# Attention scores of a 128-token tile in four visits of the tensor engine (6, 6, 4 and 4 PSUM banks) instead of five of 4

## The chip, the cores and the metric

The kernel runs on all 8 NeuronCores of one Trainium2 chip. The batch of 16 samples is split two to a core, and the cores do not talk to each other. The time is the device time in microseconds of the slowest core. The kernel before takes 2286.27 us (median of 3 runs, 2286.07 to 2286.58).

## The reference, cut to what matters

One layer: a modulated RMSNorm, one wide input projection, a pooling branch A, an attention branch B over a window of 128 tokens to either side plus 256 context keys, gates, output projection, RMSNorm and residual. The change touches the scores of branch B alone:

```python
Q_BLOCK = 128; WINDOW = 128; N_HEADS = 16; N_KV_HEADS = 4; HEAD_DIM = 64
def block(i):
    qb = q[block i]                     # (B, 128, KV, G, D)
    kb = k[blocks i-1, i, i+1]          # 384 latent keys
    s_lat = einsum('bqhgd,bkhd->bhgqk', qb, kb) * scale       # masked to |q - k| <= 128
    s_ctx = einsum('bqhgd,bkhd->bhgqk', qb, k_ctx) * scale    # 256 context keys
    p = softmax(concatenate([s_lat, s_ctx, sink_col]))
    return p_lat @ vb + p_ctx @ v_ctx
# in bf16 matmuls here; x (16, 4096, 1024), ctx (16, 256, 1024)
```

So a tile of 128 queries meets three latent blocks of 128 keys (left, own, right) and two context blocks: five key blocks. The first and the last tile of a sample have one latent block less, and so four. The left and the right block need a mask, the own block and the context blocks need none.

## The kernel before, in words

Each core works through 64 tiles (32 to a sample, two samples) in `period(p)`. All engines run programs whose order is that in which the Python code records the operations; `Tracker.emit` works out the semaphore waits. An instruction of PE (the tensor engine) never waits for another one of PE, since `_need` skips that pair. There is no scheduler: what stands first in `period` runs first on its engine. There are 8 PSUM banks of 128 x 512 f32; `next_bank` gives the one whose last use in program order is oldest.

A score visit (`visit`, matmuls at L740) treats one key block. The contraction is over 32 rows, twice (x = 0, 1, the two halves of a rotated head), so four key-value heads g = 0..3 sit in four row groups of 32 rows of the PE array and their matmuls run side by side. A visit is 8 matmuls, 512 query columns each (4 query heads x 128 queries), into 4 banks, one per g. ScalarE (ACT) then takes the exponential of each bank into the tile PT (L743), and VectorE (DVE) masks it where needed (L753), one visit later in the program (`pend`). All other matmuls use all 128 rows.

A period on PE, for tile p, in order: visit 1 (left block); K and V projection of tile p+1 (`P_kv`: 16 matmuls of 128 columns at L580, then 8 of 256 at L573); a gate block (`gm`, 8 of 512, L573); visit 2 (own block); `A_mm` (4, L804); two output blocks of tile p-2 (`out_mm`, 16, L870); visit 3 (right block); `P_xa` (32 of 128 columns, L580); a gate block; visit 4 (context 0); `P_q` (64 of 128 columns, L580); visit 5 (context 1); `B_mm` (8, L812), gate, `A_mm`; probabilities times values (`pv`, L766) with a gate block between; `B_mm`, the silu gate blocks. The right block's keys kT are made in the same period: P_kv on PE, two multiplications on DVE (L607, L609), two additions on GpSimd (POOL, L612). P_kv reads eight slices of hT that DVE writes late in the period before (`norm_mod`, L532).

Of the kernel before, what the change touches and what calls it, by code (L numbers as in the profile page):

```python
# [10 lines left out]
AF = mybir.ActivationFunctionType  # L11
# [5 lines left out]
CTX = 256  # L17
# [16 lines left out]
class Tracker:  # L34
# [27 lines left out]
                    if kn.get(k2, 0) < v2:  # L62
                        kn[k2] = v2

    def emit(self, eng, fn, reads=(), writes=(), inc=True, dma_sem=None):
        waits = {}
        self.opn += 1
        for b in reads:
            b.touch = self.opn
        for b in writes:  # L70
            b.touch = self.opn
        for b in reads:
            self._need(eng, b.last_w, waits)
            if b.excl:
                for r in b.readers:
                    if r[0] != eng:
                        self._need(eng, r, waits)
        for b in writes:
            self._need(eng, b.last_w, waits)
            for r in b.readers:  # L80
                self._need(eng, r, waits)
        self._apply_waits(eng, waits)
        if dma_sem is not None:
            self.count[dma_sem] = self.count.get(dma_sem, 0) + 16
            ev = (dma_sem, self.count[dma_sem])
            incspec = (dma_sem, 16)
        elif inc:
            self.count[eng] = self.count.get(eng, 0) + 1
            ev = (eng, self.count[eng])
            incspec = (eng, 1)  # L90
        else:
            ev = (eng, self.count.get(eng, 0) + 1)
            incspec = None
        self.snap[ev] = dict(self.known[eng])
        for b in reads:
            b.readers.append(ev)
        for b in writes:
            b.last_w = ev
            b.readers = []
        self.ops[eng].append((sorted(waits.items()), fn, incspec))  # L100
        return ev
# [61 lines left out]
def build_program(L, STOP=0):  # L163
    NT = L // 128
# [28 lines left out]
    E = tr.emit  # L193
# [6 lines left out]
    def view(t, off, dims):  # L200
        a = t[:]
        return AP(a.tensor, a.offset + off, [[a.ap[0][0], 128]] + [list(d) for d in dims])

    def pview(t, p0, pn, off, dims):
        a = t[p0:p0 + pn]
        return AP(a.tensor, a.offset + off, [[a.ap[0][0], pn]] + [list(d) for d in dims])

    with es:
# [4 lines left out]
        def sb(name, shape, dt, stack=es):  # L213
            return stack.enter_context(nc.sbuf_tensor("s_" + name, list(shape), dt))
# [17 lines left out]
        kTc = [sb(f"kTc{i}", [128, 2, CTX], BF16) for i in range(2)]  # L232
# [6 lines left out]
        qT = [sb(f"qT{i}", [128, 2, 4, 128], BF16) for i in range(2)]  # L239
        scr = [sb(f"scr{i}", [128, 512], F32) for i in range(NS)]  # L240
        ub = sb("ub", [128, 512], F32)
        kT = [sb(f"kT{i}", [128, 2, 128], BF16) for i in range(NR)]
# [9 lines left out]
        PT = sb("PT", [128, 5, 4, 512], BF16)  # L252
# [12 lines left out]
        def _lru(bufs):  # L265
            i = min(range(len(bufs)), key=lambda j: bufs[j].touch)
            tr.opn += 1
            bufs[i].touch = tr.opn
            return i

        def next_bank():
            i = _lru(pbuf)
            return pbank[i], pbuf[i]
# [3 lines left out]
        def bf(name):  # L277
            if name not in B:
                B[name] = Buf(name)
            return B[name]  # L280
# [94 lines left out]
        def gate_block(h):  # L375
# [15 lines left out]
          reads=[bf("sc"), bf("cT")], writes=[bf("sc")])  # L391
# [325 lines left out]
        def blocks_of(t):  # L717
            i = t % NT
            out = []
            if i > 0:  # L720
                out.append(("lat", (t - 1) % NR, 0))
            out.append(("lat", t % NR, None))
            if i < NT - 1:
                out.append(("lat", (t + 1) % NR, 1))
            out += [("ctx", 0, None), ("ctx", 1, None)]
            return out

        def visit(t, jb):
            kind, idx, mk = blocks_of(t)[jb]
            b = (t // NT) % 2  # L730
            q = qT[t % 2]
            banks = [next_bank() for g in range(4)]
            for x in range(2):
                for g in range(4):
                    if kind == "lat":
                        lk, kb = pview(kT[idx], 32 * g, 32, x * 128, [[1, 128]]), bf(f"kT{idx}")
                    else:
                        lk, kb = pview(kTc[b], 32 * g, 32, x * CTX + idx * 128, [[1, 128]]), bf(f"kTc{b}_{idx}")
                    rq = pview(q, 32 * g, 32, x * 512, [[1, 512]])
                    E("pe", lambda e, lk=lk, rq=rq, g=g, x=x: e.matmul(out=banks[g][0][:, :], lhsT=lk, rhs=rq, start=(x == 0), stop=(x == 1)),  # L740
                      reads=[kb, bf(f"qT{t % 2}_{x}")], writes=[banks[g][1]], inc=(x == 1))
            for g in range(4):
                E("act", lambda e, g=g: e.activation(out=PT[:, jb, g, :], in_=banks[g][0][:, :], func=AF.Exp, scale=0.125),  # L743
                  reads=[banks[g][1]], writes=[bf(f"PT{jb}_{g}")] + ([bf(f"st{jb - 2}")] if t == 0 and jb in (2, 3) else []))

        def mask(t, jb):
            mk = blocks_of(t)[jb][2]
            if mk is None:
                return
            for hh in range(2):  # L750
                v = view(PT, (jb * 4 + 2 * hh) * 512, [[128, 8], [1, 128]])
                bs = [bf(f"PT{jb}_{2 * hh}"), bf(f"PT{jb}_{2 * hh + 1}")]
                E("dve", lambda e, v=v: e.tensor_tensor(out=v, in0=v, in1=view(maskb, mk * 128, [[0, 8], [1, 128]]), op=ALU.min),  # L753
                  reads=bs + [bf("maskb")], writes=bs)
# [152 lines left out]
        def period(p):  # L907
            hasA, hasG, hasP, hasO = 0 <= p < TT, 0 <= p - 1 < TT, 0 <= p + 1 < TT, 0 <= p - 2 < TT
            nxt = p >= 0 and p + 2 < TT
            nb = len(blocks_of(p)) if hasA else 0  # L910
            visits = iter(range(nb))
            pend = []

            def vis():
                for m in pend:
                    mask(p, m)
                pend.clear()
                jb = next(visits, None)
                if jb is not None:
                    visit(p, jb)  # L920
                    pend.append(jb)

            if p == 1:
                load_gg(0)
            if hasO:
                load_res(p - 2)
            vis()
            if hasP:
                P_kv(p + 1)
            if hasG:  # L930
                tm = gm(p - 1, 7)
            vis()
            if hasG:
                u = A_mm(tm, 0)
            if hasO:
                so = [out_mm(p - 2, nb_) for nb_ in range(2)]
                out_stat(p - 2)
                if (p - 1) % NT == 0 and p - 1 < TT:
                    load_gg((p - 1) // NT)
            vis()  # L940
            if hasP:
                P_xa(p + 1)
            if hasG:
                tm = gm(p - 1, 8)
            vis()
            if hasO:
                out_evac(p - 2, so)
            if nxt:
                norm_sq()
            q = P_q(p + 1) if hasP else iter(())  # L950
            next(q, None)
            if nxt:
                norm_rs()
            next(q, None)
            if p + 2 < TT:
                load_rope(p + 2)
            vis()
# [24 lines left out]
            if hasA:  # L982
                ga(p)
                do_ybT(p)
            if hasP:
                gb(p + 1, 0)
            if nxt:
                mod_lat(p + 2, range(4, 8))
            if hasG:
                do_mgT(p - 1)  # L990
            if hasP:
                gb(p + 1, 1)
            if hasA:
                pool2(p, res)
# [54 lines left out]
        q = P_q(0)  # L1049
# [127 lines left out]
```

How the kernel before makes its waits and increments, by code:

```python
    def replay_engine(self, eng, eobj, sems):  # L121
        for waits, fn, incspec in self.ops[eng]:
            for key, val in waits:
                eobj.wait_ge(sems[key], val)
            if fn is None:
                continue
            ins = fn(eobj)
            if incspec is not None:
                ins.then_inc(sems[incspec[0]], incspec[1])
```

## Time and profile before

| | |
|---|---|
| median of 3 runs | 2286.27 us |
| profiled execution: its time | 2285.58 us |
| profiled execution: span of the slowest core | 2282.4 us |
| spans of the eight cores | 2279.7 to 2282.5 us |
| PE busy | 2229.5 us, 98% |
| DVE / ACT / POOL busy | 1446.9 / 1198.0 / 733.7 us |
| mean granted clock of PE | 0.993 to 0.994 on every core |

The execution's own time is 3.2 us above its span: what lies around the first and the last instruction. A steady period takes 33.68 us. PE's busy time counts each matmul from its start to a modelled end, so it overlaps with the next one's; the distance from one start to the next start is what a matmul really costs the stream.

### The profile page before, as it was taken

How to read it: one execution, taken by the hardware profiler on the slowest of the kernel's cores; microseconds unless marked ns; L12 is line 12 of the kernel's file. 1: busy time of each engine (PE TensorE's matmuls, PEld its weight loads, DVE VectorE, ACT ScalarE, POOL GpSimd, SP SyncE). 2: the span in 40 equal slices, each digit the busy share in tenths (PEclk: the TensorE clock that was granted, in tenths of full speed). 3: DMA queues.
4: the chain of work that ended last, by engine and by line, in shares of the span. 5: the costliest groups of instructions: out<-in, count | busy, mean ns of one | idle time of the engine just before them, and what ended most of it. 6: DMA issues, size and time to landing. Idle time of an engine off the chain costs nothing.

```text
span 2282.4 us, 64875 instructions; the slowest of 8 cores (2279.7 to 2282.5 us)
## 1 busy us (share of the span) xinstructions
PE 2229.5 (98%) x23312; PEld 1320.8 (58%) x23312; DVE 1446.9 (63%) x3896; ACT 1198.0 (52%) x2325; POOL 733.7 (32%) x852
## 2 busy tenths in 40 slices
PE   6789999999999999999999999999999999999998
PEld 1465565565565556556556556555655655655654
DVE  0456666666666666666666666666666666666664
ACT  1256556555555555555644655555555564565553
POOL 0232333333233233233333323323323323333332
PEclk9899999999999999999999999999999999999999
DMA  9991332332333343333333233334333323323312
GB/s 245 227 178 45 80 77 69 78 81 70 73 89 71 73 80 71 73 80 76 71 78 90 66 77 89 71 70 83 71 73 80 75 71 78 80 68 76 80 45 66
DMA packets 234303, 193.64 MB, mean 85 GB/s; under 512 B 197492, under 2 KB 205812, under 8 KB 231432
## 3 DMA queue, kind: packets, MB, share of 16 engines
q1 hardware_dynamic: 231544, 168.45, 31.3%
q0 software_dynamic: 2448, 21.04, 5.0%
q8 instruction: 195, 3.19, 0.6%
q14 instruction: 116, 0.95, 0.1%
HBM read 125.02 MB, written 33.56 MB: 69 GB/s over the span
## 4 chain that ended last, share of the span: by engine, by line
PE 94%; DMA 2%; DVE 1%; ACT 1%; issue 1%; POOL 0%; SPq 0%; another core or an unknown queue 0%; DVEq 0%; POOLq 0%; ACTq 0%
PE pb L573 31%; PE pb L580 23%; PE pb L812 10%; PE pb L870 10%; PE pb L740 7%; PE pb L766 6%; PE pb L804 5%; DMA s_PT<-x 2%; PE pb L354 1%; DVE s_yb L775 0%; ACT s_PT L743 0%; PE pb L526 0%; POOL s_kT L612 0%; DVE s_hT L532 0%
## 5 line engine op out<-in xcount | busy, mean ns | idle before, releaser
L573 PE MATMUL pb<-s_W,s_hT 128*128 128x512 bf16 (+1 forms) x3584 | 771.5, 364 | 0.0
L743 ACT ACTIVATE s_PT<-pb 128x512 bf16<-128x512 f32 x1264 | 652.5, 605 | 74.4 <-PE pb L740 73.6
L580 PEld LDWEIGHTS pb<-s_hT,s_W 128*128 128x128 bf16 x9216 | 525.2, 98 | 105.3 <-issue 82.7
L580 PE MATMUL pb<-s_hT,s_W 128*128 128x128 bf16 x9216 | 571.8, 220 | 1.4 <-DVE s_hT L532 0.5
L573 PEld LDWEIGHTS pb<-s_W,s_hT 128*128 128x128 bf16 x3584 | 337.9, 98 | 309.6 <-issue 1.7
L793 ACT ACTIVATE s_Tm<-pb 128x512 bf16<-128x512 f32 x256 | 153.1, 598 | 389.4 <-PE pb L573 308.3
L645 DVE TENSOR_TENSOR s_scr<-pb,s_ropet 128x512 f32<-128x512 f32 x256 | 165.0, 686 | 143.4 <-PE pb L580 142.9
L612 POOL TENSOR_TENSOR s_kT<-s_scr 128x128 bf16<-128x128 f32 x128 | 93.6, 731 | 474.7 <-DVE s_scr L609 449.8
L816 POOL TENSOR_TENSOR s_mg<-s_ub,s_scr 128x512 bf16<-128x512 f32 x128 | 161.9, 1265 | 255.3 <-DVE s_scr L797 255.3
L812 PE MATMUL pb<-s_wmf,s_ybT 128*128 128x512 bf16 x1024 | 242.5, 380 | 0.0
L775 DVE SCALAR_TENSOR_TENSOR s_yb<-pb,s_small,s_Gb 128x64 bf16<-128x64 f32 x1024 | 220.1, 277 | 28.3 <-DVE s_small L772 1.3
L870 PE MATMUL pb<-s_wmf,s_mgT 128*128 128x512 bf16 x1008 | 227.8, 379 | 0.0
L876 DVE TENSOR_TENSOR s_scr<-pb,s_gg 128x512 f32<-128x512 f32 x128 | 88.6, 692 | 182.2 <-ACT s_ttmp L873 179.4
L753 DVE TENSOR_TENSOR s_PT<-s_PT,s_maskb 128x1024 bf16<-128x1024 bf16 x248 | 181.5, 753 | 30.4 <-ACT s_PT L743 21.9
L532 DVE TENSOR_SCALAR s_hT<-s_hT,s_gs,s_sh 128x128 bf16<-128x128 bf16 x496 | 183.8, 434 | 0.0
L766 PEld LDWEIGHTS pb<-s_Vr,s_PT 128*128 128x128 bf16 x3008 | 161.9, 98 | 29.7
L797 DVE SCALAR_TENSOR_TENSOR s_ub<-s_Tm,pb 128x512 f32<-128x512 bf16 x128 | 88.0, 688 | 143.7 <-PE pb L804 135.0
L673 ACT ACTIVATE s_ttmp<-pb 128x512 bf16<-128x512 f32 x64 | 38.3, 598 | 262.4 <-PE pb L580 262.4
L650 POOL TENSOR_TENSOR s_qT<-s_scr 128x512 bf16<-128x512 f32 x128 | 160.0, 1271 | 44.3 <-DVE s_scr L645 44.3
L883 POOL TENSOR_TENSOR s_small<-s_small,s_mh 128x1 f32<-128x1 f32 x64 | 65.4, 1021 | 333.5 <-DVE s_small L881 333.5
L870 PEld LDWEIGHTS pb<-s_wmf,s_mgT 128*128 128x128 bf16 x1008 | 98.7, 98 | 118.9
L766 PE MATMUL pb<-s_Vr,s_PT 128*128 128x65 bf16 x3008 | 165.6, 193 | 0.0
(115 smaller groups left out, 2183.1 us busy)
## 6 DMA issues: line engine op xcount, KB each, us to landing
s_xr<-x SPq DMA_DIRECT2D x63, 512.0 KB, 4.9
y<-s_xr SPq DMA_DIRECT2D x63, 512.0 KB, 2.7
s_xt<-x SPq DMA_DIRECT2D x62, 512.0 KB, 4.6
s_W<-w_in POOLq DMA_DIRECT2D x10, 1024.0 KB, 32.0
s_ropet<-rope SPq DMA_DIRECT2D x64, 128.0 KB, 2.0
s_wmf<-w_mod SPq DMA_DIRECT2D x2, 2048.0 KB, 13.5
s_W<-w_mod SPq DMA_DIRECT2D x2, 2048.0 KB, 27.6
s_wmf<-w_mod POOLq DMA_DIRECT2D x2, 2048.0 KB, 17.9
```

The costliest lines, as they stand in the source:

```text
L532: E("dve", lambda e, k=k: e.tensor_scalar(out=dst[:, k, :], in0=(dst[:, k, :] if src is None else src[:, k * 128:(k + 1) * 128]), scalar1= ...
L573: E("pe", lambda e, k=k: e.matmul(out=pb[:, c0:c0 + n], lhsT=h[:, k, :], rhs=W[:, wblk, k, c0:c0 + n], start=(k == 0), stop=(k == 7)), rea ...
L580: E("pe", lambda e, c=c, k=k: e.matmul(out=pb[:, c * 128:(c + 1) * 128], lhsT=W[:, wblk, k, c * 128:(c + 1) * 128], rhs=h[:, k, :], start= ...
L645: E("dve", lambda e: e.tensor_tensor(out=view(s, 0, [[128, 4], [1, 128]]), in0=view(pbx, 0, [[128, 4], [1, 128]]), in1=view(rp, cs * 128, ...
L650: E("pool", lambda e: e.tensor_tensor(out=view(q, x * 512, [[1, 512]]), in0=a[0][:], in1=b_[0][:], op=op), reads=[a[1], b_[1]], writes=[bf ...
L743: E("act", lambda e, g=g: e.activation(out=PT[:, jb, g, :], in_=banks[g][0][:, :], func=AF.Exp, scale=0.125), reads=[banks[g][1]], writes= ...
L753: E("dve", lambda e, v=v: e.tensor_tensor(out=v, in0=v, in1=view(maskb, mk * 128, [[0, 8], [1, 128]]), op=ALU.min), reads=bs + [bf("maskb" ...
L766: E("pe", lambda e, r=r, jb=jb, rv=rv: e.matmul(out=ob[:, r * 128:r * 128 + 65], lhsT=PT[:, jb, g, r * 128:(r + 1) * 128], rhs=rv, start=( ...
L775: E("dve", lambda e, r=r, co=co: e.scalar_tensor_tensor(out=yb[:, co:co + 64], in0=ob[:, r * 128:r * 128 + 64], scalar=small[:, rc + r:rc ...
L812: E("pe", lambda e, k=k: e.matmul(out=pbk[:, :], lhsT=ybT[:, k, :], rhs=Wb[:, k, rd * 512:(rd + 1) * 512], start=(k == 0), stop=(k == 7)), ...
L816: E("pool", lambda e: e.tensor_tensor(out=mg[:, rd * 512:(rd + 1) * 512], in0=u[0][:], in1=v[0][:], op=ALU.add), reads=[u[1], v[1]], write ...
L870: E("pe", lambda e, k=k: e.matmul(out=pb[:, :], lhsT=src[:, k, :], rhs=Wo[:, k, nb * 512:(nb + 1) * 512], start=(k == 0), stop=(k == 7)), ...
```

## The change

A tile with five key blocks now has four visits. The own block has no visit any more: its query columns 0..255 of each head go along with the left block, and columns 256..511 with context block 0. Such a visit has 8 matmuls of 512 columns (`F`) and 8 of 256 (`H`) and fills 6 banks: four for F, and two in which the halves of g = 0, 1 and of g = 2, 3 lie side by side. Two row groups must not write one bank at once, so H of g = 1 and 3 runs early, and the first H of g = 0 and of g = 2 waits on PE's own semaphore until the H matmul of its partner has ended (`after`). The visits are at the places 1, 3, 4 and 5 of the period: left + half, context 0 + half, right, context 1. Nothing is left at place 2. The masks still go with the next place. ACT takes the exponentials of the halves as two instructions of 512 elements, so it has 20 to a tile as before. In the first tile of a sample place 2 is empty too, and the right block moves behind context 0. The last tile of a sample keeps its order.

```diff
-    def emit(self, eng, fn, reads=(), writes=(), inc=True, dma_sem=None):
+    def emit(self, eng, fn, reads=(), writes=(), inc=True, dma_sem=None, after=None):
         waits = {}
+        if after is not None:
+            waits[after[0]] = after[1]
...
-        def visit(t, jb):
+        def visit(t, jb, half=None):
...
+            hbanks = [next_bank() for i in range(2)] if half else []
...
+                if hb is None:
+                    bk, rq, dst = banks[g], pview(q, 32 * g, 32, x * 512, [[1, 512]]), banks[g][0][:, :]
+                    inc = x == 1
+                else:
+                    bk, rq = hbanks[g // 2], pview(q, 32 * g, 32, x * 512 + hb * 256, [[1, 256]])
+                    dst = bk[0][:, (g % 2) * 256:(g % 2) * 256 + 256]
+                    inc = x == 1
+                ev = E("pe", lambda e: e.matmul(out=dst, lhsT=lk, rhs=rq, start=(x == 0), stop=(x == 1)),
+                  reads=[kb, bf(f"qT{t % 2}_{x}")], writes=[bk[1]], inc=inc,
+                       after=done.get(g + 1) if hb is not None and g % 2 == 0 and x == 0 else None)
+                if hb is not None and g % 2 == 1 and x == 1:
+                    done[g] = ev
...
+                seq_ = [F(0, 0), H(1, 0), F(2, 0), H(3, 0), H(1, 1), H(3, 1), F(0, 1), F(1, 0), F(2, 1), F(3, 0),
+                        H(0, 0), F(1, 1), H(2, 0), F(3, 1), H(0, 1), H(2, 1)]
...
+            for g in ((0, 2, 1, 3) if half else range(4)):
...
+            if half:
+                for i in range(2):
+                    o = view(PT, (hj * 4 + 2 * i) * 512 + hb * 256, [[512, 2], [1, 256]])
+                    E("act", lambda e, i=i, o=o: e.activation(out=o, in_=view(hbanks[i][0], 0, [[256, 2], [1, 256]]), func=AF.Exp, scale=0.125),
...
-            visits = iter(range(nb))
+            if nb == 5:
+                plan = [(0, (1, 0)), None, (3, (1, 1)), (2, None), (4, None)]
+            elif p % NT == 0:
+                plan = [(0, None), None, (2, None), (1, None), (3, None)]
+            else:
+                plan = [(0, None), (1, None), (2, None), (3, None)]
```

What stands on PE at the first visit of a tile before the change; `s_kT` and `s_qT` are keys and queries, `s_hT` is the normalised input of the next tile, and the names behind "waits" are the engines waited for:

```order
L740 MATMUL pb<-s_qT,s_kT 128x512 [waits dve]
L740 MATMUL pb<-s_qT,s_kT 128x512 [waits act]
L740 MATMUL pb<-s_qT,s_kT 128x512 [waits dve] x2
L740 MATMUL pb<-s_qT,s_kT 128x512 x4
L580 MATMUL pb<-s_hT,s_W 128x128 [waits dve] x8
L580 MATMUL pb<-s_hT,s_W 128x128 x8
```

The same place with the change, to the last matmul of the visit:

```order
L753 MATMUL pb<-s_qT,s_kT 128x512 [waits dve]
L753 MATMUL pb<-s_qT,s_kT 128x256 [waits dve]
L753 MATMUL pb<-s_qT,s_kT 128x512
L753 MATMUL pb<-s_qT,s_kT 128x256 [waits act,dve]
L753 MATMUL pb<-s_qT,s_kT 128x256 x2
L753 MATMUL pb<-s_qT,s_kT 128x512 x4
L753 MATMUL pb<-s_qT,s_kT 128x256 [waits pe]
L753 MATMUL pb<-s_qT,s_kT 128x512
L753 MATMUL pb<-s_qT,s_kT 128x256 [waits pe]
L753 MATMUL pb<-s_qT,s_kT 128x512
L753 MATMUL pb<-s_qT,s_kT 128x256 x2
```

Two matmuls of 256 columns now wait for PE itself. Behind the visit stands P_kv, whose first four matmuls have lost their waits but for the first, while the next four keep one each:

```order
L582 MATMUL pb<-s_hT,s_W 128x128 [waits act,dve]
L582 MATMUL pb<-s_hT,s_W 128x128 x3
L582 MATMUL pb<-s_hT,s_W 128x128 [waits dve] x4
L582 MATMUL pb<-s_hT,s_W 128x128 x8
L575 MATMUL pb<-s_W,s_hT 128x256 x8
```

For comparison, the third visit of the core's second tile as it stands before the change, where the second matmul has no wait and the third and the fourth have one each:

```order
L740 MATMUL pb<-s_qT,s_kT 128x512 [waits act,pool]
L740 MATMUL pb<-s_qT,s_kT 128x512
L740 MATMUL pb<-s_qT,s_kT 128x512 [waits act] x2
L740 MATMUL pb<-s_qT,s_kT 128x512 x4
```

With the change this place has a context visit with half of the own block, and the right block's visit comes one place later.

The first tile of a sample on PE with the change, from its first visit on; before, the second visit stood with `s_kT` directly behind the eight matmuls of 256 columns (`s_kTc` are the context keys):

```order
L753 MATMUL pb<-s_qT,s_kT 128x512 x8
L582 MATMUL pb<-s_hT,s_W 128x128 x16
L575 MATMUL pb<-s_W,s_hT 128x256 x8
L753 MATMUL pb<-s_qT,s_kTc 128x512 x8
L582 MATMUL pb<-s_hT,s_W 128x128 x32
L753 MATMUL pb<-s_qT,s_kT 128x512 x8
L582 MATMUL pb<-s_hT,s_W 128x128 x64
L753 MATMUL pb<-s_qT,s_kTc 128x512 x8
```

The visit that needs the freshly made keys has moved behind one context visit and the 32 matmuls of P_xa.

## Rows read from the trace of the kernel before

**Rows 1.** The page, parts 1 and 4: busy time by engine, and the chain.

```profile
PE 2229.5 (98%) x23312; PEld 1320.8 (58%) x23312; DVE 1446.9 (63%) x3896; ACT 1198.0 (52%) x2325; POOL 733.7 (32%) x852
PE 94%; DMA 2%; DVE 1%; ACT 1%; issue 1%; POOL 0%; SPq 0%; another core or an unknown queue 0%; DVEq 0%; POOLq 0%; ACTq 0%
```

**Rows 2.** Timeline of PE, one period: start, length to modelled end, line, operands, count.

```profile
985.36 0.61 PE L740 MATMUL pb<-s_qT,s_kT 32*128 32x512 bf16 x8
985.90 1.19 PE L580 MATMUL pb<-s_hT,s_W 128*128 128x128 bf16 x16
...
991.03 3.62 PE L870 MATMUL pb<-s_wmf,s_mgT 128*128 128x512 bf16 x16
...
995.13 1.96 PE L580 MATMUL pb<-s_hT,s_W 128*128 128x128 bf16 x32
...
998.75 0.61 PE L740 MATMUL pb<-s_qT,s_kTc 32*128 32x512 bf16 x8
999.29 3.75 PE L580 MATMUL pb<-s_hT,s_W 128*128 128x128 bf16 x64
1002.97 0.61 PE L740 MATMUL pb<-s_qT,s_kTc 32*128 32x512 bf16 x8
...
1019.04 0.61 PE L740 MATMUL pb<-s_qT,s_kT 32*128 32x512 bf16 x8
```

**Rows 3.** Groups by form: busy us, mean ns of one.

```profile
L740 PE MATMUL pb<-s_qT,s_kTc 32*128 32x512 bf16 x1024 | 78.2, 379 | 0.0
L573 PE MATMUL pb<-s_W,s_hT 128*128 128x256 bf16 x512 | 66.4, 273 | 0.0
```

**Rows 4.** The chain of waits, 1190 to 1195 us, as start, length, what.

```profile
1192.47 0.46 POOL s_kT L612
1192.94 0.14 issue
1193.07 0.61 PE pb L740 x8
```

**Rows 5.** Timeline of PE at the third visit of the second tile.

```profile
148.75 0.84 PE L740 MATMUL pb<-s_qT,s_kT 32*128 32x512 bf16 x8 [0.35 <-POOL s_kT L612]
149.53 0.34 PE L580 MATMUL pb<-s_hT,s_W 128*128 128x128 bf16 x3
```

**Rows 6.** Timeline of PE, P_kv in three of 63 tiles, the first and last among them.

```profile
116.88 1.07 PE L580 MATMUL pb<-s_hT,s_W 128*128 128x128 bf16 x16
...
681.92 1.54 PE L580 MATMUL pb<-s_hT,s_W 128*128 128x128 bf16 x16
...
2199.64 1.22 PE L580 MATMUL pb<-s_hT,s_W 128*128 128x128 bf16 x16
```

**Rows 7.** Timeline of DVE around P_kv of rows 2.

```profile
985.30 0.98 DVE L532 TENSOR_SCALAR s_hT<-s_hT,s_gs,s_sh 128x128 bf16<-128x128 bf16 x4
```

**Rows 8.** Timeline, first tile of the core: PE, with what ended its idle time.

```profile
121.91 0.61 PE L740 MATMUL pb<-s_qT,s_kT 32*128 32x512 bf16 x8 [3.09 <-POOL s_kT L612]
...
123.33 3.46 PE L580 MATMUL pb<-s_hT,s_W 128*128 128x128 bf16 x32 [0.38 <-ACT s_PT L743]
126.72 0.68 PE L740 MATMUL pb<-s_qT,s_kTc 32*128 32x512 bf16 x8
```

**Rows 9.** Windows: busy of each engine, granted clock, DMA.

```profile
123.30:126.90 3.60, 3.57 (x36) 3.36 (x40) 1.39 (x2) 3.16 (x7) 0.00 (x0) 0.53 0.97 162
```

**Rows 10.** Timeline of ACT and PE late in the first tile.

```profile
130.48 1.05 ACT L482 ACTIVATE s_xsb<-s_xt 128x1024 bf16<-128x1024 f32 x1
...
133.97 0.61 PE L526 MATMUL pb<-s_ident,s_xsb 128*128 128x128 bf16 x8 [0.96 <-ACT s_xsb L494]
```

**Rows 11.** Timeline of PE, second visit of the second sample's first tile.

```profile
1193.07 0.61 PE L740 MATMUL pb<-s_qT,s_kT 32*128 32x512 bf16 x8 [1.29 <-POOL s_kT L612]
```

**Rows 12.** Timeline of ACT in the period of rows 2.

```profile
994.75 0.60 ACT L873 ACTIVATE s_ttmp<-pb 128x512 bf16<-128x512 f32 x1 [1.04 <-PE pb L870]
...
995.33 2.05 ACT L743 ACTIVATE s_PT<-pb 128x512 bf16<-128x512 f32 x4
```

More of the change, by code:

```diff
@@ L726, in blocks_of @@
             return out
-        def visit(t, jb):
-            kind, idx, mk = blocks_of(t)[jb]
+        def visit(t, jb, half=None):
             b = (t // NT) % 2
             q = qT[t % 2]
+            bl = blocks_of(t)
             banks = [next_bank() for g in range(4)]
[L733 to L742, printed above, removed]
-                E("act", lambda e, g=g: e.activation(out=PT[:, jb, g, :], in_=banks[g][0][:, :], func=AF.Exp, scale=0.125),
-                  reads=[banks[g][1]], writes=[bf(f"PT{jb}_{g}")] + ([bf(f"st{jb - 2}")] if t == 0 and jb in (2, 3) else []))
@@ new lines, in visit, with st, mm @@
+            hbanks = [next_bank() for i in range(2)] if half else []
+            def st(j):
+                return [bf(f"st{j - 2}")] if t == 0 and j in (2, 3) else []
+            def mm(g, x, j, hb):
+                kind, idx, mk = bl[j]
+                if kind == "lat":
+                    lk, kb = pview(kT[idx], 32 * g, 32, x * 128, [[1, 128]]), bf(f"kT{idx}")
+                else:
+                    lk, kb = pview(kTc[b], 32 * g, 32, x * CTX + idx * 128, [[1, 128]]), bf(f"kTc{b}_{idx}")
+                if hb is None:
[10 more added lines that the diff above has]
+                    done[g] = ev
@@ new lines, in visit @@
+            done = {}
+            if half is None:
+                seq_ = [(g, x, jb, None) for x in range(2) for g in range(4)]
+            else:
+                hj, hb = half
+                F = lambda g, x: (g, x, jb, None)
+                H = lambda g, x: (g, x, hj, hb)
+                seq_ = [F(0, 0), H(1, 0), F(2, 0), H(3, 0), H(1, 1), H(3, 1), F(0, 1), F(1, 0), F(2, 1), F(3, 0),
+                        H(0, 0), F(1, 1), H(2, 0), F(3, 1), H(0, 1), H(2, 1)]
+            for a in seq_:
+                mm(*a)
@@ new lines, in visit @@
+            for g in ((0, 2, 1, 3) if half else range(4)):
+                E("act", lambda e, g=g: e.activation(out=PT[:, jb, g, :], in_=banks[g][0][:, :], func=AF.Exp, scale=0.125),
+                  reads=[banks[g][1]], writes=[bf(f"PT{jb}_{g}")] + st(jb))
+            if half:
+                for i in range(2):
+                    o = view(PT, (hj * 4 + 2 * i) * 512 + hb * 256, [[512, 2], [1, 256]])
+                    E("act", lambda e, i=i, o=o: e.activation(out=o, in_=view(hbanks[i][0], 0, [[256, 2], [1, 256]]), func=AF.Exp, scale=0.125),
+                      reads=[hbanks[i][1]], writes=[bf(f"PT{hj}_{2 * i}"), bf(f"PT{hj}_{2 * i + 1}")] + st(hj))
@@ L910, in period @@
             nb = len(blocks_of(p)) if hasA else 0
-            visits = iter(range(nb))
+            if nb == 5:
+                plan = [(0, (1, 0)), None, (3, (1, 1)), (2, None), (4, None)]
+            elif p % NT == 0:
+                plan = [(0, None), None, (2, None), (1, None), (3, None)]
+            else:
+                plan = [(0, None), (1, None), (2, None), (3, None)]
+            visits = iter(plan)
             pend = []
@@ L917, in vis @@
                 pend.clear()
[L918 to L921, printed above, removed]
+                v = next(visits, None)
+                if hasA and v is not None:
+                    visit(p, *v)
+                    pend.append(v[0])
             if p == 1:
```

## The prediction

> **What bounds the kernel now.** I read the page's busy times and chain first: PE is busy for 98% of the span and is 94% of the chain [rows 1]. So the time is PE's stream of instructions, and an edit is worth what it does to the distances between starts in it. The timeline of PE shows these distances. Columns stream at 56 ns for a 128-wide matmul ((1.96 - 0.22)/31) and 216 ns for a 512-wide one ((3.62 - 0.38)/15) [rows 2]. A visit's eight matmuls are two rounds of four side by side: 0.61 us to the modelled end, less 0.37 to 0.38 for one matmul, puts the second round 0.23 us behind the first. The next block starts 0.54 us after the visit (998.75 to 999.29), 0.11 more than two rounds of 0.216. On the way in, 64 matmuls from 999.29 would be through at 1002.88, and the visit starts at 1002.97: 0.10 more [rows 2]. So a visit costs 0.64 us, of which 0.43 is columns and 0.21 is the change between 128-row and 32-row work. Five are 3.2 us of the period's 33.68.
>
> **The removed visit.** The columns stay, since the own block is moved and not dropped. Without any new cost, a six-bank visit is 3 x 0.216 + 0.21 = 0.86 us, and a tile has 2 x 0.86 + 2 x 0.64 = 3.00 instead of 3.20: 0.2 us less. That is what the change can win per tile.
>
> **The waits of PE on itself.** Count from the visit's first matmul. F of g = 0 starts at 0, H of g = 1 beside it, its second H (the one waited for) when the 256 columns are through, at 0.12. No row shows a 32-row matmul of 256 columns. The 128-row one lasts 0.273, the 512-wide 32-row one 0.379 [rows 3], 0.106 less gives the same 0.27, so it ends at 0.39. How fast PE goes on after a semaphore is seen where nothing is queued: GpSimd's kT ends at 1192.94, and the visit starts 0.14 later [rows 4]. No row shows PE waiting for PE. From below the cost is zero (if the wait were met in the background), from above it is this full restart, and I take the restart, since a wait stands in PE's instruction stream whoever signals. The first H of g = 0 then starts at 0.39 + 0.14 = 0.53. Its row group is free at 0.43 to 0.44. **That is a stall of 0.10.** All four groups are stopped, as the instructions behind it cannot pass.
>
> The second wait, for g = 2, is long met by then, but it is not free. In the second tile's third visit the queue had run dry on kT, and the third and fourth matmul had a met wait each: there the visit lasts 0.84 instead of 0.61, and the next block starts after 0.78 instead of 0.54 [rows 5, 2]. That is 0.12 for each met wait once PE has nothing queued. So H of g = 2 starts at 0.66, and F of g = 3, the last full one, behind it at 0.67 instead of 0.44. Usually the next block starts 0.31 after the last round (0.54 - 0.23), which makes 0.98, and with 0.10 on the way in **a six-bank visit costs 1.07 us instead of the ideal 0.86**. It has to stay below 1.5 x 0.64 = 0.96 to win anything. The rows also show that groups may run out of step, as these did in [rows 5], so I let H and F overlap.
>
> **P_kv behind the first visit.** Sixteen matmuls with no stall take 1.07 us, as in the first of [rows 6]. In the steady period they take 1.19 [rows 2], in the worst quiet stretch 1.54, at the end 1.22 [rows 6], and the mean over the 63 is 1.24: 0.17 of stall per tile. The reason is DVE, which rewrites the last four slices of hT until 986.28 [rows 7], just when PE reads them. DVE's work hangs on the gate blocks ahead of the visit, so with P_kv starting 0.43 later it is done in time, and this stall goes even where it was 0.47. What is late next: four of P_kv's matmuls keep a wait each. With nothing queued these come 0.12 apart, while the matmuls are 56 ns apart. From the visit's last two matmuls on, the fourth wait is met about 0.05 too late. So P_kv costs 0.05 instead of 0.17.
>
> **Sum for one tile of five blocks.** Place 1: +0.43 (1.07 - 0.64) and -0.12. Place 3: +0.43. Place 2: -0.64. Together +0.10 to +0.11 us. There are 60 such tiles (30 in a sample): +6.5 us.
>
> **First tiles.** In the first tile of all, visit 2 stands idle 3.09 us for kT [rows 8]. Behind it P_xa takes 3.46 us for the 32 matmuls that take 1.96 in rows 2, as the granted clock fell to 0.53 of full speed there (the 1.2 GHz level) after that idle time [rows 9, 8]. With the context visit in its place, kT is wanted only about 0.6 us before it is ready (the context visit and P_xa, 0.64 + 1.8, stand in the 3.09), and P_xa runs at full clock. PE would be 4.2 us ahead, but a later step limits it: the transpose at 133.97 waits for ACT's normalisation, whose first part starts at 130.48 behind the exponentials of the visits [rows 10]. These start and end about 4 us earlier too; I count 3.9. In the second sample's first tile the wait of 1.29 for kT goes [rows 11]: 1.3. The second tile's wait (0.35 and the two late waits, 0.24, [rows 5]) goes too, as the right block is now at place 4: 0.6. Together -5.8 us, once.
>
> **What costs nothing.** The exponentials are 20 of 0.52 us (2.05 for four) as before. The second six-bank visit comes 8.9 us after the first, about 994.3; ACT is then busy with the square of the second output block until about 995.1 (now from 994.75 [rows 12]) and would finish six exponentials at 998.2. The next four banks are wanted at 998.9, and they are the ones evacuated first, by 997.3. So 1.6 us cover that. The banks of P_kv and of the gate block behind it come from the two silu gate blocks. DVE has done the first one's gate before it turns to the slices of hT, and does the second one's next after 986.28 [rows 7]; these banks are wanted at 986.3 and 988.2. The right block's mask moves behind P_q's multiplications on DVE, and pv reads it more than 1 us later. If one of these covers went, it would cost what it lacks, 60 times.
>
> Total: +6.5 - 5.8 = +0.7 us. In the profile's own terms 2285.6 becomes 2286.3 and the span 2283.1; the median of the runs was 0.7 above the profiled time, so I predict 2287 us. The likely error of the per-tile sum is 0.1 us, which is 6 us: the likeliest case alone is 2280 to 2294.
>
> **Rivals.**
>
> *The waits are cheap.* PE might take its own signal faster than another engine's, or the met wait might cost less than in rows 5. For it: both prices come from other releasers. Against: the place in the instruction stream is the same. Without the 0.12 of the second wait a tile is at +0.11 - 0.24 = -0.13, so -8 - 6: 2272. With both free, place 1 costs +0.22 and P_kv -0.17, place 3 +0.22, place 2 -0.64: -0.37 a tile, -22 - 6: 2258. Chance 0.2 together, mostly the former.
>
> *The groups do not run out of step with a 256-wide matmul.* If the H beside an F holds its row group until the F is through, the H waited for starts at 0.22 instead of 0.12, and everything behind it is 0.10 later: 2 x 0.10 x 60 = 12 us, thus 2299. For it: all matmuls side by side are 512 wide in this trace. Against: rows 5, where groups were 0.12 and 0.25 apart. It decides the sign if it costs over 0.04 a visit. The Trainium skill ("TensorE: Matmul & The Clock Gate", section on packing small matmuls by row and column tiling) says that matmuls keep program order in their start and in their end; taken strictly, a short H could not end ahead of the F issued before it. By that rule it is this case. The trace neither shows nor excludes it. Chance 0.13.
>
> *Banks or ACT.* Six banks at once leave two for P_kv and the gate block. If evacuation were late by 0.2 to 0.4 us in each tile, this is 12 to 24 us: 2299 to 2311. Against: the margins above are 0.9 us and more. Chance 0.07.
>
> *The visit count does not matter,* that is, the 0.21 for changing over grows with the number of matmuls. Then nothing is saved at place 2 beyond its columns: +0.2 a tile, 2299. The 0.54 and the 0.10 are the same at both kinds of visit, so I see little for it; it is in the upper tail.
>
> **How the numbers follow.** The forecast has 0.6, the rivals 0.2, 0.13 and 0.07. I count within 0.2% (4.6 us) as the same, about what a measurement of this kernel can tell. The forecast's own spread of 7 us leaves 0.4 inside, 0.08 faster, 0.12 slower. With the rivals: faster 0.27, same 0.41, slower 0.32. For 8 in 10 the range goes from 2268, which takes in the first rival's nearer half, to 2302, which takes in the second.
>
> **What would show it.** In the changed profile the two six-bank visits should be 1.0 us from their first matmul to the next block's, with a gap of 0.1 before the first H of g = 0 and 0.12 between it and the H of g = 2. P_kv's 16 matmuls should take about 1.12. The steady period should be 33.8. The wait for kT in the first tile should be under 0.7 us and the half-clock stretch behind it gone. I am wrong if the visits take under 0.9 (the waits are cheap) or over 1.05 (groups in step), or if PE waits for ACT or DVE anywhere in the steady period.

## The result, and the profile after

The changed kernel takes **2342.42 us** (median of 6 runs, the lowest 2342.13), the kernel before 2286.17 beside it. The ratio is 1.0246, 95% interval 1.0235 to 1.0257: 56 us slower. The forecast was 2287, with a range from 2268 to 2302. In some runs the cores of one die get a lower clock and the time is longer; the times of the experiments below are medians of the other runs. The steady period is 34.70 us (1006.98 to 1041.68 below) and not 33.8; it was 33.68 [rows 2].

The page of the changed kernel, parts 1 and 4 [rows 1]:

```profile
PE 2272.8 (97%) x23792; PEld 1367.4 (58%) x23792; DVE 1538.5 (66%) x3896; ACT 1190.3 (51%) x2325; POOL 733.3 (31%) x852
PE 89%; DVE 5%; DMA 2%; issue 2%; ACT 1%; POOL 0%; another core or an unknown queue 0%; SPq 0%; DVEq 0%; POOLq 0%; ACTq 0%
```

DVE has gone from 1% to 5% of the chain, and has 92 us more of busy time with the same 3896 instructions. Part 5 names them:

```profile
L786 DVE TENSOR_TENSOR s_PT<-s_PT,s_maskb 128x1024 bf16<-128x1024 bf16 x248 | 289.9, 1209 | 0.0
L652 POOL TENSOR_TENSOR s_qT<-s_scr 128x512 bf16<-128x512 f32 x128 | 187.9, 1489 | 45.5 <-DVE s_scr L647 45.5
```

The mask multiplications take 1209 ns on average, where they took 753 in the kernel before (its line 753). GpSimd's combination of q takes 1489 and took 1271. The list of waits (engine and line that waits, what it waits for, us in total, times, longest) starts for PE with a wait that is not in the list of the kernel before:

```profile
PE pb L582 <- DVE s_Gb L669: 18.7, 57, 0.7
...
PE pb L799 <- DVE s_PT L786: 2.2, 1, 2.2
...
PE pb L753 <- POOL s_kT L614: 0.7, 1, 0.7
```

The timeline of PE, one period, answers to [rows 2]:

```profile
1006.98 1.08 PE L753 MATMUL pb<-s_qT,s_kT 32*128 32x512 bf16 x16
1008.35 1.55 PE L582 MATMUL pb<-s_hT,s_W 128*128 128x128 bf16 x16 [0.28 <-DVE s_Gb L669]
...
1016.75 0.38 PE L753 MATMUL pb<-s_qT,s_kTc 32*128 32x512 bf16 x1
...
1016.76 0.39 PE L753 MATMUL pb<-s_qT,s_kT 32*128 32x256 bf16 x3
...
1017.32 0.27 PE L753 MATMUL pb<-s_qT,s_kT 32*128 32x256 bf16 x1
...
1017.44 0.27 PE L753 MATMUL pb<-s_qT,s_kT 32*128 32x256 bf16 x1
...
1017.77 1.96 PE L582 MATMUL pb<-s_hT,s_W 128*128 128x128 bf16 x32
...
1041.68 1.08 PE L753 MATMUL pb<-s_qT,s_kT 32*128 32x512 bf16 x16
1043.05 1.16 PE L582 MATMUL pb<-s_hT,s_W 128*128 128x128 bf16 x9 [0.29 <-DVE s_Gb L669]
```

The second six-bank visit, at 1016.75, is about as forecast: 1.02 us to the next block. The first takes 1.37 to P_kv, which waits 0.28 for a bank, and P_kv then takes 1.55 instead of 1.12. Together that is 0.35 + 0.43 = 0.8 us a tile, in the place where I had counted on a gain. What delays DVE starts 15 us earlier, at the end of the tile before. DVE:

```profile
1025.79 1.29 DVE L647 TENSOR_TENSOR s_scr<-pb,s_ropet 128x512 f32<-128x512 f32 x2 [0.35 <-PE pb L582]
1026.99 3.13 DVE L786 TENSOR_TENSOR s_PT<-s_PT,s_maskb 128x1024 bf16<-128x1024 bf16 x2
1030.05 0.68 DVE L830 SCALAR_TENSOR_TENSOR s_scr<-s_Tm,pb 128x512 f32<-128x512 bf16 x1
1032.25 0.69 DVE L830 SCALAR_TENSOR_TENSOR s_ub<-s_Tm,pb 128x512 f32<-128x512 bf16 x1 [1.53 <-POOL s_mg L849]
...
1042.22 0.69 DVE L669 SCALAR_TENSOR_TENSOR s_Gb<-s_ttmp,pb 128x512 bf16<-128x512 bf16 x1 [0.92 <-PE pb L753]
1042.82 0.98 DVE L534 TENSOR_SCALAR s_hT<-s_hT,s_gs,s_sh 128x128 bf16<-128x128 bf16 x4
```

The profile puts the 0.92 us before Gb down to PE's visit, which is older. Gb reads ACT's tanh, and that ends at 1042.05, right behind the gate Ga:

```profile
1041.45 0.60 ACT L668 ACTIVATE s_ttmp<-pb 128x512 bf16<-128x512 f32 x1 [2.46 <-DVE s_Ga L676]
```

GpSimd:

```profile
1026.62 2.95 POOL L652 TENSOR_TENSOR s_qT<-s_scr 128x512 bf16<-128x512 f32 x2 [0.49 <-DVE s_scr L647]
1030.87 1.27 POOL L849 TENSOR_TENSOR s_mg<-s_ub,s_scr 128x512 bf16<-128x512 f32 x1 [1.29 <-DVE s_scr L830]
```

The same two engines in the kernel before, DVE first, with the right block's masks at 996.51 and 997.49:

```profile
996.51 0.69 DVE L753 TENSOR_TENSOR s_PT<-s_PT,s_maskb 128x1024 bf16<-128x1024 bf16 x1
997.49 0.69 DVE L753 TENSOR_TENSOR s_PT<-s_PT,s_maskb 128x1024 bf16<-128x1024 bf16 x1 [0.28 <-ACT s_PT L743]
...
1008.19 0.69 DVE L797 SCALAR_TENSOR_TENSOR s_ub<-s_Tm,pb 128x512 f32<-128x512 bf16 x1 [1.90 <-PE pb L804]
```

```profile
1003.98 2.50 POOL L650 TENSOR_TENSOR s_qT<-s_scr 128x512 bf16<-128x512 f32 x2 [0.49 <-DVE s_scr L645]
```

**Theory M (the late mask).** With the right block third in the order of visits, its mask comes at place 5, behind P_q's multiplications. There it runs beside GpSimd's combination of q, and two multiplications, which take 1.28 together where nothing is beside them (e3), take 3.13. So B_mm's gate starts at 1030.05, GpSimd's sum mg behind it ends at 1032.14, and A_mm's gate, which rewrites ub that this sum reads, has to wait for it. Before, that gate waited for PE. DVE's outputs behind pv, the gate Ga, ACT's tanh and the first gate Gb follow later; Gb has the bank that P_kv needs, and the last slices of hT are behind Gb.

**Rivals.** Theory B: six banks at once are too many, and the bank of Gb would be late wherever the mask is. Theory W: the cost is in PE's waits on its own signal (a matmul that waits for another matmul).

One number separates the kernels below: how long before the next tile's first visit DVE starts A_mm's gate (the ub row). It is 10.85 us before the change (1008.19 to 1019.04) and 9.43 after it (1032.25 to 1041.68).

### The profile page after: what moved, and what is told of

It is laid out like the page before. It is cut to its first block, busy times and chain, and to the rows that moved or that the text cites. A ratio compares the mean times of both kernels' runs of the same rounds, so it can differ in the third digit from the quotient of the medians.

```text
span 2340.6 us, 65730 instructions; the slowest of 8 cores (2338.3 to 2340.6 us)
## 1 busy us (share of the span) xinstructions
PE 2272.8 (97%) x23792; PEld 1367.4 (58%) x23792; DVE 1538.5 (66%) x3896; ACT 1190.3 (51%) x2325; POOL 733.3 (31%) x852
## 4 chain that ended last, share of the span: by engine, by line
PE 89%; DVE 5%; DMA 2%; issue 2%; ACT 1%; POOL 0%; another core or an unknown queue 0%; SPq 0%; DVEq 0%; POOLq 0%; ACTq 0%
PE pb L575 29%; PE pb L582 24%; PE pb L903 9%; PE pb L845 9%; PE pb L753 7%; PE pb L799 6%; PE pb L837 5%; DMA s_PT<-x 2%; DVE s_Gb L669 2%; DVE s_yb L808 1%; PE pb L356 1%; DVE s_hT L534 0%; DVE s_PT L786 0%; ACT s_ttmp L668 0%
## 5 line engine op out<-in xcount | busy, mean ns | idle before, releaser
L582 PE MATMUL pb<-s_hT,s_W 128*128 128x128 bf16 x9216 | 588.1, 219 | 20.8 <-DVE s_Gb L669 18.7
L771 ACT ACTIVATE s_PT<-pb 128x512 bf16<-128x512 f32 x1024 | 528.3, 605 | 73.0 <-PE pb L753 72.0
L786 DVE TENSOR_TENSOR s_PT<-s_PT,s_maskb 128x1024 bf16<-128x1024 bf16 x248 | 289.9, 1209 | 0.0
L652 POOL TENSOR_TENSOR s_qT<-s_scr 128x512 bf16<-128x512 f32 x128 | 187.9, 1489 | 45.5 <-DVE s_scr L647 45.5
L668 ACT ACTIVATE s_ttmp<-pb 128x512 bf16<-128x512 f32 x128 | 76.5, 597 | 233.8 <-DVE s_Ga L676 138.1
L906 ACT ACTIVATE s_ttmp<-pb 128x512 bf16<-128x512 f32 x128 | 76.4, 597 | 193.0 <-PE pb L903 193.0
L675 ACT ACTIVATE s_ttmp<-pb 128x512 bf16<-128x512 f32 x64 | 38.2, 597 | 264.1 <-PE pb L582 264.1
L753 PE MATMUL pb<-s_qT,s_kT 32*128 32x256 bf16 (+1 forms) x1984 | 162.2, 327 | 1.0 <-POOL s_kT L614 0.7
```

Of the source, the lines that this page charges most:

```text
L582: E("pe", lambda e, c=c, k=k: e.matmul(out=pb[:, c * 128:(c + 1) * 128], lhsT=W[:, wblk, k, c * 128:(c + 1) * 128], rhs=h[:, k, :], start= ...
L652: E("pool", lambda e: e.tensor_tensor(out=view(q, x * 512, [[1, 512]]), in0=a[0][:], in1=b_[0][:], op=op), reads=[a[1], b_[1]], writes=[bf ...
L753: ev = E("pe", lambda e: e.matmul(out=dst, lhsT=lk, rhs=rq, start=(x == 0), stop=(x == 1)), reads=[kb, bf(f"qT{t % 2}_{x}")], writes=[bk[1 ...
```

## The experiments

The masks' place and the visits were taken apart first. The kernel before was run beside each group of four, and losses are counted against it: 2288.05 us beside e1 to e4, 2286.07 beside e5 to e8, 2286.85 beside e9 to e12. The changed kernel, with 2286.17 beside it, lost 56.2.

**e1: right block at place 3, its mask at place 4.**

```diff
-                plan = [(0, (1, 0)), None, (3, (1, 1)), (2, None), (4, None)]
+                plan = [(0, (1, 0)), None, (2, (1, 1)), (3, None), (4, None)]
```

> The changed kernel with the right block back at place 3 (with the second half of the own block) and context 0 at place 4, so that the right block's mask runs at place 4 again, while GpSimd is idle, and not beside GpSimd's combination of q. Theory M (the moved mask is slowed by GpSimd and makes DVE late for P_kv): the masks are 0.69 us again, P_kv starts 1.0 us after the visit and takes about 1.1, the steady period is 33.8, the time about 2287 (range 2278 to 2296). Rival B (the six banks: P_kv's bank now comes from a later gate, however DVE stands): P_kv still waits 0.3 or more for DVE's gate, time 2310 or more. Rival W (PE's waits on itself are what costs): nothing changes, about 2342.

Measured: 2298.6 us, ratio 1.0046 (1.0028 to 1.0064). The loss is 10.6 instead of 56.2, so 46 us are gone, with all six-bank visits still there, so B falls. The visit is undisturbed and P_kv near the forecast (timeline of PE):

```profile
1025.78 1.08 PE L753 MATMUL pb<-s_qT,s_kT 32*128 32x512 bf16 x16
1026.79 1.15 PE L582 MATMUL pb<-s_hT,s_W 128*128 128x128 bf16 x16
```

**e2: the kernel before, five visits of four banks, with only the order changed** so that the mask comes as late as in the changed kernel.

```diff
-            visits = iter(range(nb))
+            visits = iter([0, 1, 3, 2, 4] if nb == 5 else range(nb))
```

> The kernel before, with its five visits of four banks, in the order left, own, context 0, right, context 1: only the right block's place changes, and with it that its mask runs behind P_q's multiplications. Theory M: the masks take 1.2 to 1.7 us and most of the 55 us comes, about 0.8 us a tile: 2325 to 2340. Rivals B and W: no six-bank visit and no wait of PE on itself here, so the time stays at 2286 within 5.

Measured: 2356.53 us, ratio 1.03 (1.0284 to 1.0316): a loss of 68.5, more than the changed kernel's and more than was expected. Not one matmul is added, so W is no cause of the large loss. DVE first, then PE:

```profile
1000.09 3.14 DVE L753 TENSOR_TENSOR s_PT<-s_PT,s_maskb 128x1024 bf16<-128x1024 bf16 x2
...
1005.35 0.69 DVE L797 SCALAR_TENSOR_TENSOR s_ub<-s_Tm,pb 128x512 f32<-128x512 bf16 x1 [1.52 <-POOL s_mg L816]
```

```profile
1014.78 0.61 PE L740 MATMUL pb<-s_qT,s_kT 32*128 32x512 bf16 x8
1015.32 0.40 PE L580 MATMUL pb<-s_hT,s_W 128*128 128x128 bf16 x4
1016.38 1.33 PE L580 MATMUL pb<-s_hT,s_W 128*128 128x128 bf16 x12 [0.66 <-DVE s_hT L532]
```

The ub gate starts 9.43 before the visit, as in the changed kernel. PE reaches P_kv 0.43 earlier here, and so waits more: 1.29 a tile on average. The longer first visit hides part of the delay; it does not cause it.

**e3: the changed kernel, the masks of five-block tiles between P_q's two halves.**

```diff
             next(q, None)
+            if nb == 5:
+                for m in pend:
+                    mask(p, m)
+                pend.clear()
```

> The changed kernel with its visits as they are; only the two mask instructions of the right block are put between the two halves of P_q on DVE, before GpSimd combines q. Theory M: most of the loss goes, 2290 to 2305, as the masks are 0.7 us again but push the second pair of P_q's multiplications and the combination of q back by up to 1.4 us. Rivals B and W: about 2342.

Measured: 2298.88 us, ratio 1.0047 (1.0031 to 1.0063). Same order of visits as the changed kernel, and the loss is 10.8 instead of 56.2: 45 us less. Both masks take 1.28 together, and the ub gate starts 10.54 before the visit (1024.73):

```profile
1008.26 1.28 DVE L786 TENSOR_TENSOR s_PT<-s_PT,s_maskb 128x1024 bf16<-128x1024 bf16 x2
...
1014.19 0.69 DVE L830 SCALAR_TENSOR_TENSOR s_ub<-s_Tm,pb 128x512 f32<-128x512 bf16 x1 [1.77 <-POOL s_mg L849]
```

**e8: half of the mask late,** the other half between P_q's halves.

```diff
+            if nb == 5 and pend == [2]:
+                mask(p, 2, (0,))
+                pend[:] = [(2, (1,))]
```

> The changed kernel with one of the right block's two mask instructions between the two halves of P_q and the other one at its late place. If the masks beside GpSimd's combination of q are the cause and DVE's delay adds up to PE's, about half of the 44 us between the two forms is left or somewhat less, as the first microsecond of delay has slack: 2305 to 2325. If only both together, or something else, cost: 2299 or 2342.

Measured: 2295.47 us, from a single run, so no ratio can be given. The expected half of the loss did not come. The profile agrees with that run: the late mask takes 1.45, the ub gate starts 10.70 before the visit (1022.79), and P_kv takes 1.09.

```profile
1008.17 1.45 DVE L786 TENSOR_TENSOR s_PT<-s_PT,s_maskb 128x1024 bf16<-128x1024 bf16 x1
...
1012.09 0.69 DVE L830 SCALAR_TENSOR_TENSOR s_ub<-s_Tm,pb 128x512 f32<-128x512 bf16 x1 [1.87 <-POOL s_mg L849]
```

GpSimd:

```profile
1007.80 2.95 POOL L652 TENSOR_TENSOR s_qT<-s_scr 128x512 bf16<-128x512 f32 x2
1010.72 1.26 POOL L849 TENSOR_TENSOR s_mg<-s_ub,s_scr 128x512 bf16<-128x512 f32 x1
```

So the loss is not proportional to the late work. With one late mask, B_mm's gate ends at 1010.22 (it starts behind the mask, at 1009.54), before GpSimd is through with q, and mg starts without waiting for DVE. With two, mg stood idle 1.29 for that gate (the row at 1030.87 above). The second late mask is the one that goes past DVE's slack.

**e9: the changed kernel without GpSimd's combination of q from the third tile on.** It leaves out a part of the computation, so its q is stale from there on. This asks whether the mask's place alone is enough, or whether it needs GpSimd beside it.

```diff
             def comb(x, a, b_, op):
+                if t >= 2:
+                    return
```

> The changed kernel, masks at their late place, but GpSimd's two instructions that combine q (L652) are left out from the third tile on, so q is stale there: part of the computation is left out. It tells GpSimd's traffic from the mere place of the masks. Theory M with contention as its cause: the masks are 0.69 us each, end 0.3 us after B_mm's result, and the loss goes: about 2298. If the place alone delays DVE enough (1.4 us of masks in front of the gate): 2320 or more.

Measured: 2296.97 us, ratio 1.0043 (1.0025 to 1.0061). The masks are at the same late place and take 1.28:

```profile
1009.80 1.28 DVE L788 TENSOR_TENSOR s_PT<-s_PT,s_maskb 128x1024 bf16<-128x1024 bf16 x2
...
1013.64 0.69 DVE L832 SCALAR_TENSOR_TENSOR s_ub<-s_Tm,pb 128x512 f32<-128x512 bf16 x1 [1.96 <-PE pb L839]
```

The place alone does not bring the loss; it needs GpSimd beside it. (That GpSimd is also free sooner here explains nothing: in the changed kernel it was idle before mg already.)

**e10: the changed kernel, A_mm's product into the ring of scratch tiles instead of ub.** This leaves the slow masks and takes away only the wait for the sum mg.

```diff
-            return gate_mul(tm, pa, pab, ub, bf("ub"))
+            return gate_mul(tm, pa, pab, *(next_scr() if rd else (ub, bf("ub"))))
```

> The changed kernel with its late masks, and the gated product of the second A_mm goes to the ring of four scratch buffers and not to the one buffer ub, so DVE doesn't wait for GpSimd's sum to read ub (the wait of 1.5 us at L830). If this link carries the delay from the masks to the pv results and on to P_kv: DVE is 1.5 us earlier there, PE's wait goes and the time is about 2298. If the masks' own length is enough to make DVE late: 2325 to 2342.

Measured: 2296.11 us, ratio 1.0041 (1.0026 to 1.0056). The masks are as slow as ever, and the loss is gone all the same:

```profile
1008.93 3.13 DVE L786 TENSOR_TENSOR s_PT<-s_PT,s_maskb 128x1024 bf16<-128x1024 bf16 x2
1011.98 1.47 DVE L830 SCALAR_TENSOR_TENSOR s_scr<-s_Tm,pb 128x512 f32<-128x512 bf16 x2
...
1023.31 0.69 DVE L669 SCALAR_TENSOR_TENSOR s_Gb<-s_ttmp,pb 128x512 bf16<-128x512 bf16 x1 [0.92 <-ACT s_ttmp L668]
```

The second gate follows the first at once and is through at 1013.45, where the changed kernel's started 1.5 us after the first had ended. The visit is at 1023.62, so Gb starts 0.31 ahead of it, and in the changed kernel 0.54 behind it. Both links are thus needed for the loss: slow masks, and a buffer that turns DVE's delay into a wait for GpSimd and back.

Four kernels then ask what the visits themselves cost.

**e4: e1 with one wait in a visit instead of two** (for the last signal, which covers the other).

```diff
-                       after=done.get(g + 1) if hb is not None and g % 2 == 0 and x == 0 else None)
+                       after=done.get(3) if hb is not None and g == 0 and x == 0 else None)
```

> As the run with the right block at place 3, and the first H matmul of g = 0 waits for the partner of g = 2 too (the later of the two), so the second wait of PE on itself goes. If a met wait with nothing queued costs 0.12 us: the six-bank visits take 0.88 us instead of 1.0 and the time is 14 us less than in that run, about 2273. If a met wait is free: no difference beyond 2 us.

Measured: 2287.96 us, ratio 0.9997 (0.9987 to 1.0008), 10.6 less than e1. A visit is 0.93 instead of 1.02, so the met wait costs 0.09 and not 0.12:

```profile
1022.70 1.00 PE L753 MATMUL pb<-s_qT,s_kT 32*128 32x512 bf16 x16
1023.63 1.07 PE L582 MATMUL pb<-s_hT,s_W 128*128 128x128 bf16 x16
```

**e5: e4 with the last full matmuls ahead of the wait; e6: the same sequence with both waits.**

```diff
-                        H(0, 0), F(1, 1), H(2, 0), F(3, 1), H(0, 1), H(2, 1)]
+                        F(1, 1), F(3, 1), H(0, 0), H(2, 0), H(0, 1), H(2, 1)]
```

> As the run with one wait of PE on itself (right block at place 3), and in a six-bank visit the two last full matmuls (F of g = 1 and 3) stand ahead of the waiting H matmuls instead of behind them. If the stall costs only because the full matmuls queue behind it, the visit falls from 0.93 to about 0.85 us, 120 times: 10 us less than the run with one wait, about 2278, and below the kernel before. If the waits cost by their mere number, no change: 2288.

> The same order with both waits of PE on itself kept. The second wait then delays only two H matmuls of 256 columns, so it costs 0.08 to 0.12 of the visit's end: visit about 0.93 to 0.97, time 2288 to 2292. If the order hides it: 2278.

Measured: e5 2284.69 us, ratio 1.0007 (0.9985 to 1.0028; one run of 2305.33 is in it and widens it); e6 2295.07, ratio 1.0041 (1.0025 to 1.0056). Both are above what was expected. A visit of e5 still takes 0.93, as in e4, not the 0.85 expected:

```profile
1018.21 0.99 PE L753 MATMUL pb<-s_qT,s_kT 32*128 32x512 bf16 x16
1019.14 1.17 PE L582 MATMUL pb<-s_hT,s_W 128*128 128x128 bf16 x16
```

In both orders the H matmuls behind the wait start at 0.60 and later, and they are the last to start (0.73 in both); the full ones moved ahead, at 0.45, were not what ended the visit. The second wait costs e6 its 10 us again.

**e7: the kernel before, only the order in the first tile of a sample changed.**

```diff
-            visits = iter(range(nb))
+            visits = iter([0, None, 2, 1, 3] if nb == 4 and p % NT == 0 else range(nb))
```

> The kernel before with the new order of visits in the first tile of each sample alone (left out at place 2, right block at place 4), everything else as before. The prediction's term: 3.9 + 1.3 = 5.2 us less (the second tile's 0.6 isn't in it): 2281 to 2282 where the kernel before has 2286 to 2288. If later waits eat the gain: no difference.

Measured: 2282.18 us, ratio 0.9984 (0.9972 to 0.9995): a gain of 3.9, not 5.2.

**e11: e7, with the last four slices of hT ahead of the first silu gate block; e12: e5 with the same.** They remove the stall of P_kv [rows 6, 7] directly.

```diff
-            if hasP:
-                gb(p + 1, 0)
             if nxt:
                 mod_lat(p + 2, range(4, 8))
+            if hasP:
+                gb(p + 1, 0)
```

> The kernel before with the new order in the first tiles of the samples alone, and the last four slices of hT written by DVE before the first silu gate and not behind it. This takes away the 0.17 us for which P_kv waits for these slices in each tile: P_kv's 16 matmuls take 1.07 us and the time falls by 5 to 10 us, to 2273 to 2278. If another wait takes its place (the gate's bank, ACT's buffer): no difference to the run with the first tiles alone, 2283.

> The form with six-bank visits, one wait of PE on itself and the full matmuls first, with the same early slices of hT. P_kv loses only 0.08 us to waits in that form, and these are PE's own, so the early slices bring nothing: 2283 to 2286. Then the five visits are the better form by 8 us.

Measured: **e11 2272.48 us, ratio 0.9938 (0.992 to 0.9956)**, as expected, the fastest of all and faster than both kernels; e12 2281.67, ratio 0.9977 (0.9967 to 0.9988). P_kv of e11 runs with no stall in the steady period:

```profile
981.36 1.07 PE L580 MATMUL pb<-s_hT,s_W 128*128 128x128 bf16 x16
```

In e12 P_kv takes 1.07 on average too, and the time is 3 us under e5's, where I had expected nothing. In e1 the stall is 0.06 even in the 46 tiles of 60 whose slices are all written before P_kv starts, so most of the 0.08 are met waits. With the slices ahead of the gate, P_kv's wait for the gate's bank covers them, and these waits go too.

With that stall gone in both, five visits of four banks beat the best four-visit form tried by 9.2 us, 0.15 a tile. The visits account for it: a six-bank visit of e12 is 0.94 on average, with 0.10 on the way in 1.04, and two of these less three of 0.64 are 0.16. So this is what the change itself costs, with the mask and the second wait out of it.

## Why the prediction was wrong

**The step that failed** is in "What costs nothing": "The right block's mask moves behind P_q's multiplications on DVE, and pv reads it more than 1 us later." I asked only when the mask is read. I did not ask what runs beside it on GpSimd, nor what is queued behind it on DVE. The runs showed a cost of 45 us of the 56 measured (e3 against the changed kernel, each against the kernel before beside it), where the sum had nothing. The neighbouring claim, that the bank from the first silu gate is free when P_kv wants it, held only while DVE was on time: in the changed kernel this gate ends at 1042.91, where P_kv could have started at 1042.70 (1.02 behind the visit). The traces had the warning. In the kernel before, 122 masks run beside the combination of k and half of these take 0.95 instead of 0.69, and the combination of q follows right on P_q's multiplications, where I was putting the mask. The list of line 753 before, and of line 786 after (duration ns min, median, max):

```profile
L753 DVE TENSOR_TENSOR s_PT<-s_PT,s_maskb x248: 681/693/951, 123.8 to 2236.3; 128x1024 bf16<-128x1024 bf16 x124
```

```profile
L786 DVE TENSOR_TENSOR s_PT<-s_PT,s_maskb x248: 680/1196/1764, 128.3 to 2294.1; 128x1024 bf16<-128x1024 bf16 x124
```

The Trainium skill ("SBUF — State Buffer", section "SBUF: two separate sides") names this pair: a DVE operation with two SBUF inputs and a GpSimd operation that reads SBUF exclude each other on a shared port pair. It also says that the one that starts second is blocked for the other's whole instruction. This trace agrees with both. One instruction at a time, the rows of the changed kernel are:

```profile
1026.62 1.27 POOL L652 TENSOR_TENSOR s_qT<-s_scr 128x512 bf16<-128x512 f32 x1 [0.49 <-DVE s_scr L647]
1026.99 1.45 DVE L786 TENSOR_TENSOR s_PT<-s_PT,s_maskb 128x1024 bf16<-128x1024 bf16 x1
1027.85 1.72 POOL L652 TENSOR_TENSOR s_qT<-s_scr 128x512 bf16<-128x512 f32 x1
1028.36 1.76 DVE L786 TENSOR_TENSOR s_PT<-s_PT,s_maskb 128x1024 bf16<-128x1024 bf16 x1
```

The first combination takes the 1.27 that it takes alone, although a mask starts inside it. That mask ends at 1028.44, 0.55 behind the combination's end at 1027.89. The second combination then takes 1.72, 0.45 more than alone, and the second mask ends at 1030.12, again 0.55 behind the combination's end. In all 62 such tiles of this trace both distances are 0.546 to 0.554. So the two engines take turns, one whole instruction each. A mask alone takes 0.69, so 0.14 of it does not wait for the turn; which part that is, the rows do not show.

The rest, without the mask (e1, e3), is +10.7 us, where I had +0.7:

- *The removed visit and the changing over:* right. The lead-in of 0.10 and the 0.54 behind a four-bank visit are as before.
- *PE's own signal, and the met wait:* the mechanism is right, the sum 0.04 small. I had 0.53 to the first H of g = 0, the row shows 0.57 (1016.75 to 1017.32). The one of g = 2 is 0.12 behind it, as said. The visit is 1.02 (median) and on average 1.04 instead of 0.98: 0.06 x 120 = 7 us. This is the largest of the small terms. e4 prices the second wait at 10.6 us; I had 14. Of the 7, 5 us are the later first H (0.04 a visit), the rest is that some visits are longer than the median.
- *Waits are cheap:* wrong, the visit is not under 0.9 even with one wait.
- *Groups in step:* not borne out. Three 256-wide matmuls take 0.39 from the first start to the last end (1016.76), where one takes 0.27. So the last of them starts 0.12 behind the first, ahead of the end of the 512-wide ones beside it; in step it would be 0.22. The visit is under the 1.05 that I gave as the limit.
- *Banks or ACT:* the wait for the bank of Gb did come, and at 0.8 us a tile it is larger than this rival had it. But it comes from the mask. With the mask back in its place no wait for Gb's bank is left in P_kv (1.15 in e1), so six banks cost nothing of this kind.
- *P_kv:* 0.08 (e1) and 0.09 (e3) of stall on average, not 0.05: 2 us. Where the slices are ready it is 0.06; in a quarter of e1's tiles DVE still comes late.
- *First tiles:* the waits for kT went, as forecast (4.7 us in 3 waits before, 0.7 in one after). But pv came earlier too, and now waits 2.2 us for DVE's mask (the list of waits above), and the granted clock then fell to 0.50, the 1.2 GHz level, in pv. The half-clock stretch of [rows 9] did not go, it moved. e7 gives 3.9 us for these tiles instead of 5.2, 1 us less. The window of the changed kernel (the third number from the end is the granted clock):

```profile
130.90:133.30 2.40, 1.98 (x37) 1.78 (x34) 1.98 (x10) 0.58 (x1) 2.26 (x2) 0.50 0.96 171
```

7 + 2 + 1 = 10 us, the 10 by which the rest was off.

## What to carry to other kernels

An instruction that is moved on a side engine has three prices: when its result is read, which instruction of GpSimd it will have to take turns with there, and who is queued behind it; "read a microsecond later" answers only the first. A buffer that two engines hand to and fro (ub here) turns a small delay of one into a wait of both, and another buffer removed that wait here with no new one to be seen (e10). Splitting a step so as to save a change of mode has to be set against the waits on the engine's own signals that it brings: here one change less saved 0.21 us a tile, and the waits cost that and more.

## What the runs showed of the hardware

- Two bf16 multiplications of DVE with both inputs in SBUF take 1.28 us beside an idle GpSimd (e3, e9) and 3.13 beside its additions of f32 tiles; GpSimd's pair goes from 2.50 to 2.95. The engines take turns, a whole instruction each, and whichever comes second waits. Before the change it was GpSimd that lost to the same masks: its s_small of one element a partition took 1.10 us (median, line 883) and takes 0.55 now that they are elsewhere (line 916).
- PE that waits for a signal of its own goes on 0.57 us after the visit's start, 0.45 after the start of the matmul that gives the signal (0.12). Matmuls moved ahead of the wait do not shorten the visit (e4 and e5: 0.93 both). A second wait, already met, costs 0.09 us more.
- What ends the idle time in the list of waits is the last link only: "DVE s_Gb" 18.7 us was caused 15 us before each of these waits, and changing either of two other instructions (e9, e10) removed it.

What stays open: e8 rests on one run and its profile, so the size of DVE's slack is known only as between one late mask and two. Nor do the rows show which 0.14 us of a mask escape the turn. e11 was not combined with e10's buffer, nor with the right block's mask at a place free of GpSimd's work on k.
